# Expert rows gathered one block further ahead, softmax sums inverted in the attention stage, and w_out loaded from GpSimd's queue

## The reference, cut to what matters

```
y_att = dsa_attention(...)                     # 8 heads x 64: softmax over selected keys
hm    = mlstm_chunkwise(...)                   # 4 heads x 128, y_mlstm = sigmoid(mo) * rmsnorm(hm)
merged = sigmoid(ga) * (y_att @ w_proj_att) + sigmoid(gm) * (y_mlstm @ w_proj_mlstm)
x1 = x + merged @ w_out
xn = rmsnorm(x1) ; top-1 group of 4, top-2 of its 8 experts per token
# routed_experts: tokens sorted by expert, padded to blocks of 128 rows
hid = silu(xblk @ w_gate[e]) * (xblk @ w_up[e]);  yblk = hid @ w_down[e]
out = x1 + sum over the two experts of gate * y
```

## Time and profile before

| | |
|---|---|
| median of 3 runs (lowest to highest) | 3448.9 us (3448.4 to 3451.57) |
| profiled execution, its own time | 3453.41 us |
| its span | 3451.8 us |
| mean granted TensorE clock of it | 0.946 |
| PE busy | 3007.7 us, 87% |
| DVE / ACT / POOL busy | 72% / 53% / 13% |
| merge and output stage | about 1909 to 2390 us of the span |
| expert blocks | about 2434 to 3368 us |

### The profile page before, as it was taken

One profiled execution on the slowest core, in us unless ns is written; L12 is line 12 of the kernel. 1 busy time (PEld: TensorE's weight loads), 2 busy tenths in 40 slices (PEclk: granted clock), 3 DMA queues, 4 the chain that ended last, 5 costly groups with the idle time before them and its releaser, 6 DMA issues. The chain is left out here.

```text
span 3451.8 us, 45088 instructions
## 1 busy us (share of the span) xinstructions
PE 3007.7 (87%) x12983; PEld 2230.6 (65%) x12984; DVE 2482.7 (72%) x3906; ACT 1815.0 (53%) x2523; POOL 446.2 (13%) x587
## 2 busy tenths in 40 slices
PE   6998699799899968999899589996699999999980
PEld 5765578588688634554455377775577777777760
DVE  5577588789989866676653335443898989889874
ACT  5322467576678434443334223332577777777760
POOL 0211110100000042212111000000111111111113
PEclk9999899999999979999999789998799999999995
DMA  3222322222222274454422556543569779666868
GB/s 122 81 72 67 105 82 71 65 75 73 68 65 74 71 180 126 115 111 96 85 71 51 161 164 189 166 152 110 200 245 368 273 287 348 232 226 254 312 266 346
DMA packets 367695, 536.99 MB, mean 156 GB/s; under 512 B 35632, under 2 KB 201040, under 8 KB 367424
## 3 DMA queue, kind: packets, MB, share of 16 engines
q1 hardware_dynamic: 338288, 430.70, 39.9%
q0 software_dynamic: 26960, 96.13, 7.6%
q10 hardware_dynamic: 2304, 8.39, 0.6%
HBM read 510.18 MB, written 129.80 MB: 185 GB/s over the span
## 5 line engine op out<-in xcount | busy, mean ns | idle before, releaser
L906 DVE TENSOR_TENSOR e_w_lo<-e_raw,e_w_hi 128x1024 fp32r<-128x1024 f32 x386 | 446.9, 1219 | 3.0 <-ACT e_w_hi L768 3.0
L1558 PE MATMUL x_ps<-h_hi,x_w_hi 128*128 128x512 f32 (+1 forms) x1024 | 402.1, 393 | 0.0
L1558 PE MATMUL x_ps<-h_lo,x_w_hi 128*128 128x512 f32 (+1 forms) x1024 | 401.1, 392 | 0.0
L1558 PE MATMUL x_ps<-h_hi,x_w_lo 128*128 128x512 f32 (+1 forms) x1024 | 401.1, 392 | 0.0
L768 ACT CAST e_w_hi<-e_raw 128x1024 fp32r<-128x1024 f32 x386 | 376.9, 1053 | 5.0 <-PE e_pG L710 5.0
L1748 DVE TENSOR_SCALAR_CACHE_REDUCE x_relu<-x_score,x_cand 128x1024 uint8<-128x1024 f32 (+3 forms) x217 | 315.6, 1487 | 3.6
L1661 ACT ACTIVATE x_relu<-x_score,x_cand 128x896 int8<-128x896 f32 (+3 forms) x217 | 281.0, 1296 | 56.4 <-DVE x_cand L1755 56.2
L2316 DVE CUSTOM_DVE_ANT_0 t_junk<-t_L,t_mask 128x512 bf16<-128x512 f32 (+3 forms) x320 | 185.7, 607 | 166.7 <-PE t_L L2098 165.7
L2137 PE MATMUL t_O<-t_probT,t_v 128*65 128x512 f32 x544 | 289.4, 614 | 13.8 <-ACT t_probT L2288 12.5
L2288 ACT ACTIVATE t_probT<-t_ST 128x512 f32<-128x512 f32 x272 | 160.4, 593 | 261.5 <-PE t_ST L2129 260.9
L710 PE MATMUL e_pG<-e_w_hi,e_x_hi 128*128 128x512 f32 x768 | 246.8, 402 | 3.6 <-DVE e_x_lo L901 3.6
(11 more groups left out here) (404 smaller groups left out, 6204.7 us busy)
## 6 DMA issues: line engine op xcount, KB each, us to landing
e_raw<-in_w_exp_gate SPq DMA_DIRECT2D x392, 256.0 KB
e_raw<-in_w_exp_up SPq DMA_DIRECT2D x392, 256.0 KB
e_raw<-in_w_exp_down SPq DMA_DIRECT2D x192, 512.0 KB
projT<-x_out SPq DMA_DIRECT2D x124, 256.0 KB
slot_out<-e_y POOLq DMA_DIRECT2D x48, 512.0 KB, 6.1
o_gate<-projT SPq DMA_DIRECT2D x32, 512.0 KB
x_w_raw<-in_w_in SPq DMA_DIRECT2D x31, 512.0 KB
a_tables<-in_x SPq DMA_DIRECT2D x16, 512.0 KB, 4.8
```

The costliest lines, as they stand in the source:

```text
L906: nc.vector.tensor_tensor(w_lo[:, u, :], raw[:, u, :], w_hi[:, u, :].bitcast(F32), ALU.subtract).then_inc(gl, 1)
L1558: last = nc.tensor.matmul(ps[0:w, u % 4, :], wt[:, m % 2, kk, 0:w], ht[:, kk, q * 512:(q + 1) * 512], start=(kk == 0 and s == 0), stop=(kk ...
```

## The change

Three edits.

1. Inverse sums. The attention stage loads the sums of query groups 0 to 2 back as each group ends (`t_sums`, one [128, 32] tile each), DVE inverts them there, SP stores them to `inverse_sums`. Only group 3 is left to the merge stage, whose SP list loads it late and stores it after group 0's merges.
2. The merge stage's SP list. `inverses(0)` comes right behind the first rows, `w_out` moves to POOL's list (with the same wait on `wl`), `gates(1)` goes ahead of the y_attT rows, and the five loads of constants (gain, router weights, biases) move from before the loop to behind `gates(3)`.
3. Experts. POOL gathers block 2 in front of its loop, and in the loop the gather of block n + 2 instead of n + 1; it waits for the landing of n + 1 and the transposes of n. `IX` has one more column of zeros for the one gather more.

```
@@ merge_and_output, SP
-            sp.dma_start(SUM[:, :], pg.d["exp_sums"].rearrange(...)).then_inc(sum_in, 16)
+            last = lambda d: d[:, (NGRP - 1) * W:].rearrange("h (a b) -> h a b", b=32)
             proj_weights(0)
             rows(0, ORDER[:4])
+            inverses(0)
             gates(0)
             proj_weights(1)
-            sp.wait_ge(rec_ok, 1)
-            sp.dma_start(rec_d.rearrange(...), SUM[:, :]).then_inc(rec_st, 16)
-            sp.wait_ge(rec_st, 16)
-            inverses(0)
+            gates(1)
             rows(0, ORDER, 4)
-            gates(1)
-            (five loads of constants)
-            for k in range(2):
-                w_out(k)
+            sp.dma_start(SUM[:, :], last(pg.d["exp_sums"])).then_inc(sum_in, 16)
             for g in range(NGRP):
                 for m in range(KT):
                     u = g * KT + m
-                    if g == 0 and m + 2 < KT:
-                        w_out(m + 2)
                     if u + 2 <= LASTM:
                         proj_weights(u + 2)
                         gates(u + 2)
+                    if u == 1:
+                        (five loads of constants)
                 if g == 0:
+                    sp.wait_ge(rec_ok, 1)
+                    sp.dma_start(last(rec_d), SUM[:, :]).then_inc(rec_st, 16)
                     sp.wait_ge(wl, KT)
@@ merge_and_output, POOL
+            for k in range(KT):
+                if k >= 2:
+                    pool.wait_ge(wl, k - 1)
+                pool.dma_start(X[:, k % 2, :], i["w_out"][k * P:(k + 1) * P, :]).then_inc(w_in[k % 2], 16)
@@ merge_and_output, DVE: the reciprocal moves from the list's head to behind rows(0, range(4, 8))
@@ route_and_experts, POOL
+            pool.wait_ge(x_in, 32)
+            pool.wait_ge(xt_ps, 1)
+            indices(2, 0)
+            gather(2, 0)
...
-                        pool.wait_ge(x_in, 16 * n + 16)
-                        pool.wait_ge(xt_ps, n)
-                        indices(n + 1, b)
-                        gather(n + 1, b)
+                        pool.wait_ge(x_in, 16 * n + 32)
+                        pool.wait_ge(xt_ps, n + 1)
+                        indices(n + 2, 1 - b)
+                        gather(n + 2, 1 - b)
                         store(n - 1)
@@ attend_and_recur, SP (after the stores of step s)
+                    if v == 0 and n % 4 == 0 and n:
+                        for b in range(3):
+                            sp.wait_ge(y_st[b], 48 * len(range(b, s, 3)))
+                        sp.dma_start(SUM[:, n // 4 - 1, :], sums(sum_d, n // 4 - 1)).then_inc(sum_in, 16)
+                    if v == 0 and n % 4 == 2 and n > 4:
+                        sp.wait_ge(rec_ok, n // 4)
+                        sp.dma_start(sums(rec_d, n // 4 - 1), SUM[:, n // 4 - 1, :]).then_inc(rec_st, 16)
@@ attend_and_recur, DVE
+                    if j == 0 and v == 1 and n % 4 == 1 and n > 4:
+                        dve.wait_ge(sum_in, 16 * (n // 4))
+                        v_.reciprocal(SUM[:, n // 4 - 1, :], SUM[:, n // 4 - 1, :]).then_inc(rec_ok, 1)
```

More of the change, by code:

```diff
@@ L136, in merge_and_output @@
         y_hi, y_lo = sb("y_hi", [P, 8, W], F32R), sb("y_lo", [P, 8, W], F32R)
-        SUM, YR, REC = sb("sums", [P, AH * SEQ // P]), sb("y", [P, 4, W]), sb("inverse", [P, 4, W])
+        SUM, YR, REC = sb("sums", [P, 32]), sb("y", [P, 4, W]), sb("inverse", [P, 4, W])
         PR = sb("p", [P, 2, 8, P])
@@ L154, in merge_and_output @@
         g_in = [sem(f"gate_in{b}") for b in range(2)]
-        w_in = [sem(f"w_in{k}") for k in range(2)]
+        w_in = [pg.sw_sem(f"o_w_in{k}") for k in range(2)]
         x_in = [sem(f"x_in{b}") for b in range(2)]
@@ L200, in inverses @@
                     sp.wait_ge(yl, 8 * g)
+                if g == NGRP - 1:
+                    sp.wait_ge(rec_st, 16)
                 for z in range(2):
@@ L234, in _ @@
                         gates(u + 2)
+                    if u == 1:
+                        sp.dma_start(G[:, :], i["g_norm_moe"].partition_broadcast(P)).then_inc(consts, 16)
+                        sp.dma_start(WR[:, :, 0:NG], i["w_router_group"].rearrange("(k p) n -> p k n", p=P)).then_inc(consts, 16)
+                        sp.dma_start(WR[:, :, NG:NR], i["w_router_expert"].rearrange("(k p) n -> p k n", p=P)).then_inc(consts, 16)
+                        sp.dma_start(BI[:, 0, 0:NG], i["b_router_group"].partition_broadcast(P)).then_inc(consts, 16)
+                        sp.dma_start(BI[:, 0, NG:NR], i["b_router_expert"].partition_broadcast(P)).then_inc(consts, 16)
                 if g == 0:
+                    sp.wait_ge(rec_ok, 1)
+                    sp.dma_start(last(rec_d), SUM[:, :]).then_inc(rec_st, 16)
                     sp.wait_ge(wl, KT)
@@ L394, in output @@
                                        op0=ALU.mult, op1=ALU.mult).then_inc(xn_ok, 1)
-            dve.wait_ge(sum_in, 16)
-            v.reciprocal(SUM[:, :], SUM[:, :]).then_inc(rec_ok, 1)
             proj_weights(0)
@@ L400, in _ @@
             rows(0, range(4, 8))
+            dve.wait_ge(sum_in, 16)
+            v.reciprocal(SUM[:, :], SUM[:, :]).then_inc(rec_ok, 1)
             for g in range(NGRP):
@@ L625, in _ @@
             g.memset(ones[:, :], 1.0)
-            g.memset(IX[:, NBLK:NBLK + 1], 0)
+            g.memset(IX[:, NBLK:NBLK + 2], 0)
             g.memset(lt[:, :], 1.0).then_inc(r_set, 1)
@@ L658, in _ @@
                     with pool.If(n < used):
-                        pool.wait_ge(x_in, 16 * n + 16)
-                        pool.wait_ge(xt_ps, n)
-                        indices(n + 1, b)
-                        gather(n + 1, b)
+                        pool.wait_ge(x_in, 16 * n + 32)
+                        pool.wait_ge(xt_ps, n + 1)
+                        indices(n + 2, 1 - b)
+                        gather(n + 2, 1 - b)
                         store(n - 1)
             store(end)
-            pool.wait_ge(x_in, 16 * used + 16)
+            pool.wait_ge(x_in, 16 * used + 32)
             pool.wait_ge(y_st, 16 * used + PRIMED)
@@ L1800, in attend_and_recur @@
     qk_d = pg.dram("qkT", (2 * MH, P, SEQ))
-    sum_d = pg.dram("exp_sums", (AH, SEQ))
+    sum_d, rec_d = pg.dram("exp_sums", (AH, SEQ)), pg.dram("inverse_sums", (AH, SEQ))
+    NGRP = SEQ // 512
     RW = MH * NT
@@ L1832, in unit_at, with sums @@
         return UNITS_AT.index(f - off) if f - off in UNITS_AT else None
+    def sums(d, g):
+        return d[:, g * 512:(g + 1) * 512].rearrange("h (a b) -> h a b", b=32)
     def ended(f, off):
@@ L1850, in attend_and_recur @@
         B2 = c.enter_context(nc.psum_tensor("t_B2", [P, 2, 512], F32))
+        SUM = sb("sums", [P, NGRP - 1, 32])
+        sum_in, rec_ok, rec_st = sem("sum_in"), sem("rec_ok"), sem("rec_st")
         gF, gI, ge, gl, gb, gd, gc, gM = (sb("g_" + n, [RW, P]) for n in ("F", "I", "e", "l", "b", "d", "cm", "M"))
@@ L2009, in _ @@
                 sp.wait_ge(y_st[b], 48 * len(range(b, len(STEPS), 3)))
+            sp.wait_ge(rec_st, 16 * (NGRP - 1))
             for b in range(2):
```

15 lines of the change are left out of this document (2 added, 13 removed).

## The result

| | before | after |
|---|---|---|
| median of the runs in the comparison, us | 3450.2 (3448.4 to 3457.3, 4 runs) | 3425.9 (3420.6 to 3430.0, 4 runs) |
| profiled execution, us (span) | 3453.4 (3451.8) | 3430.0 (3428.1) |
| mean granted clock of it | 0.946 | 0.943 |

The ratio is 0.992, with a 95% interval of 0.9906 to 0.9934. Of the 52 us of the forecast's sum, 23 came (3453.4 to 3430.0 in the profiled executions).

The account below looks back on a forecast made before the run. The prediction took PE as the bound, with waits at the merge stage's start and for expert gathers. Terms 29 + 23 + 1.5 - 0.5 - 1 = 52 us took 3453.4 to 3401.4, or 3397 for the median; range 3384 to 3420.

Parts of the forecast that it names:

- Gather, 29 us: Expert blocks: gathering one block ahead ends PE's waits for late gathers; 29 us gained, bounds 18 and 30.
- Rival A: Expert blocks: weights take the gather's place, changing blocks stay at 18.5 us; about 11 us lost, 3408; chance 0.15.
- w_out and the seven merges, 23 us: Merge stage, group 0: w_out on POOL's queue cuts seven merges from 73.01 to 50 us; 23 gained, bounds 11 and 31.
- Rival B: Merge stage: merges stay paced by transfers, 8.9 us per slice; 12 us lost, 3409; chance 0.18.
- Inverses early, 1.5 us gained: Merge stage's start: the 12 us chain goes but the queue fills; 1.5 us gained, bounds -2 and 8.
- Product and the rows of group 1, 1 us lost: End of group 0: the last group's sums are stored in front of the next group's rows; 1 us lost, bounds 0 and 2.
- The small things in attention, 0.5 us lost, bounds 0 and 3: Attention stage: three small inversions beside PE's work and SP's waits for stores long landed; 0.5 us lost in all.
- The two small terms of the merge stage: Merge stage: early inverses, 1.5 us gained, and sums stored before the next group's rows, 1 us lost.
- Rival D: Attention stage: new waits of SP and DVE delay loads and maxima; price over 52 us, 3455; chance 0.02.

Follow-up runs that it names:

- experiment 4: The kernel before with the gather's part of the change alone: 3418.6 us, ratio 0.9904.
- Experiment 7: The kernel of experiment 2 with group 1's attention rows and inverses issued behind the gates of slice 8: 3397.7 us, ratio 0.9871.
- experiment 2: The changed kernel with the DRAM tensor `inverse_sums` allocated behind the small tensors of the mLSTM gate rows: 3401.4 us, ratio 0.9857.
- experiment 5: The kernel before with an unused 64 KB DRAM tensor ahead of `m_neg_rows` and `inter_rows`, no instruction changed: 3467.2 us, ratio 1.0069.

## Why the prediction was wrong

Its own steps, one by one:

- **Gather, 29 us: right.** 30.9 us in the profiles, 31 alone in experiment 4. Rival A is out: blocks at a DMA share of 1.04 last 18.11 us like the others. That is 0.3 us less than the 18.4 worked out from 7.34 MB and 398 GB/s, so a block's bytes were overcounted or reach into its neighbours.
- **w_out and the seven merges, 23 us: right, with some luck.** 49.6 us where 50 was forecast. The forecast had 10.9 us of idle PE (2.87 + 3 + 5) at a clock near 1.00; there were 8.1, and PE's work took 41.6 us at a clock of 0.93, against 39.0 in group 1. The two deviations, 2.9 and 2.5 us, nearly cancel. The gap at slice 4 was 6.3 us (forecast 5), from the constants. Rival B is out, since four of the other six merges follow each other without a gap.
- **Inverses early, 1.5 us gained: wrong in sign, small.** The chain over store and reload went, but the rows landed 23.6 us after the first issue (23.3 before), as the queue was full (share 1.03). Merge 0 ended 32.5 us after that issue (31.2 before), so 1.3 us were lost. The prediction had seen the queue fill and forecast the same landing. Its gain was to come from the rows arriving one after the other, so that DVE's 2.65 us would partly overlap; but DVE made its four products in 2.71 us in one go behind the landing, as before.
- **Product and the rows of group 1, 1 us lost: 4.65.** The step looked at one store's issue. What moved was the order: the loads of group 1 were issued 8.8 us after the last merge (3.5 before), because SP first waits for DVE's `gated(7)`, and DVE's list has `p_lo` of the next weights ahead of it. Experiment 7 moved those loads and gave 3 us back in the stage; then the rows of x were late, behind the same wait.
- **The small things in attention, 0.5 us lost, bounds 0 and 3: this step failed, by 21 us.** It counted instructions and waits: those cost 0.7 us on SP, and nothing in the stage (696.2 us in experiment 2, with all of them in place). It did not count that a tensor allocated 64 KB long, ahead of two others, moves them. `inter_rows` left the one place where its rows were read from two regions; its load then took 3 us more in each of 16 chunks. DVE's waits for it grew from 11.0 to 26.5 us, POOL's from 90.5 to 133.1, DVE's 64 `t_m_AR` from 28.1 to 39.0 us of busy time, and PE's for `t_m_T` from 11.9 to 35.8. Experiments 2 and 5 take the loss away from after and put it into before by this place alone.

With that step right the rest of the sum holds: experiment 2 is the whole change without the shift, and its ratio of 0.9857 (0.9843 to 0.9871) contains the forecast's 3397 / 3448.9 = 0.985 (48 of the 52 us). The two small terms of the merge stage were off by 2.8 and 3.7 us, the gather by 1.9 the other way. Rival D had the right stage and a wrong mechanism. It sought the danger in waits and gave it 0.02; the condition that the prediction named for being wrong, the attention stage moving by more than 3 us, is what happened.

The longer `t_m_AR` (669 ns on average against 498 ns) can be read from the traces. Of its 64 in before, the 52 that ran beside no instruction of POOL took 336 to 348 ns; the 12 that ran beside POOL's `t_m_QW` or `t_m_T` took 1174 on average. In after, 27 of the 64 overlap one (1116 ns) and 37 do not (336 to 349 ns). A late `t_m_WI` makes DVE and POOL start together, and so more of them overlap. Why an overlap makes them longer is not shown.

What stays open is why reads of one region are limited. The runs show only that they are, by which offsets, and that multiples of 64 KB (after and experiment 5) and of 128 KB (one case, +112 KB) do not help.

## What to carry to other kernels

A diff moves more than instructions: list which DRAM and on-chip tensors get another address, and for every small source that is spread to many partitions ask where its rows lie. A load whose landing time changes in every repetition, the first included, while its queue is the same, may have moved rather than been delayed; one line of padding in the old kernel tests that for the price of one run. Rows that are read together and often may be laid 256 KB apart: that was worth 40 us to the changed kernel (3425.9 to 3386.4). Some 24 of these only undo the loss of the shift, as experiment 2 does; 15 go beyond it (3401.4 to 3386.4).

## What the runs showed of the hardware

- A load that spreads four 512 B rows of DRAM to 128 partitions (256 KB written) took 10.2 to 11.0 us from issue to landing, behind 1 MB of other loads, with all four rows inside one 256 KB region; 7.2 and 7.5 us with them on both sides of a multiple of 256 KB; 5.1 us with each in a region of its own. A load of the same 256 KB from distinct addresses (`t_m_X`), issued ahead of it, took 4.3 to 4.7.
- Moving on-chip tiles by 384 B changed nothing (0.9998, 0.9989 to 1.0008).
- DVE's `t_m_AR` (128x128) took 336 to 349 ns alone and 1.1 to 1.2 us on average beside an instruction of POOL (before and after).
- Issuing 5 small constant loads from SP between others held SP up to 5.38 us at one issue.
- DMA moved 397 to 399 GB/s in single expert blocks of 18.11 us with PE never waiting.
